# Hybrid decoder block on one core: softmax statistics merged on 16 partitions, and squares of q and k summed from two fp32r parts

## What is computed

```python
hmix = rmsnorm(x, norm_mix_g); proj = hmix @ w_in
q = rmsnorm(qkv[:, :, 0], q_norm_g) * scale      # per head, 64 channels: needs the sum of squares
k = rmsnorm(qkv[:, :, 1], k_norm_g)
for g, (window, dilation) in enumerate(((128, 1), (512, 4), (2048, 16))):
    o_g, lse_g = dilated_window_attention(q[g], k[g], v[g], slopes[g], window, dilation)
wgt = softmax(stack(lses), axis=0)                # over the three patterns, per token and head
o_attn = sum(wgt[..., None] * stack(outs), axis=0)
```

## Time and profile before

| what | us |
|---|---|
| median of 3 runs | 1832.22 (1832.21 to 1833.08) |
| time of the profiled execution | 1834.04 |
| its span, first to last instruction | 1832.2 |
| TensorE busy in the span | 1787.6 (98%) |
| mean granted TensorE clock | 0.994 |

### The profile page before, as it was taken

The page is one execution under the profiler, slowest core; times in us unless marked ns, Lnnn a source line. Parts: engine busy times, 40 slices in busy tenths (PEclk is TensorE's granted clock), DMA queues, the critical chain, the costliest instruction groups (busy, mean ns, idle before and its releaser), DMA issues.

```text
span 1832.2 us, 23655 instructions
## 1 busy us (share of the span) xinstructions
PE 1787.6 (98%) x8628; PEld 1420.1 (78%) x8628; DVE 1023.9 (56%) x1545; ACT 562.1 (31%) x1069; POOL 828.9 (45%) x597
## 2 busy tenths in 40 slices
PE   8999999999999987999999999999999999999997
PEld 6777777777777766788888888788888888888786
DVE  6336645564655489343313323787787887544644
ACT  6533444354245423111411222533333333000000
POOL 7536443644544274664225734265455454222221
PEclk9999999999999999999999999999999999999999
DMA  4111111211121023444411244322222232445211
GB/s 173 36 41 48 52 53 41 64 53 41 41 58 47 24 70 91 107 116 123 165 58 70 93 145 167 135 86 87 69 96 76 69 103 92 138 150 193 81 55 49
DMA packets 64194, 158.11 MB, mean 86 GB/s; under 512 B 10912, under 2 KB 27680, under 8 KB 64112
## 3 DMA queue, kind: packets, MB, share of 16 engines
q1 hardware_dynamic: 51856, 145.35, 24.4%
q10 hardware_dynamic: 11792, 10.04, 2.0%
q0 software_dynamic: 464, 1.62, 0.2%
HBM read 123.54 MB, written 32.26 MB: 85 GB/s over the span
## 4 chain that ended last, share of the span: by engine, by line
PE 88%; DVE 7%; POOL 1%; issue 1%; DMA 1%; ACT 1%; SPq 0%; DVEq 0%; POOLq 0%
PE bank L911 14%; PE bank L913 13%; PE bank L912 13%; PE bank L1274 7%; PE bank L1276 7%; PE bank L1275 7%; PE bank L1332 4%; PE bank L1334 4%; PE bank L1333 4%; PE bank L925 2%; PE bank L1059 2%; PE bank L1072 2%; PE bank L1045 2%; DVE run_z L1772 1%; PE bank L1238 1%
## 5 line engine op out<-in xcount | busy, mean ns | idle before, releaser
L911 PE MATMUL bank<-hhi,whi 128*128 128x512 f32 x1024 | 420.7, 411 | 5.8 <-DVE hlo L1709 4.0
L912 PE MATMUL bank<-hlo,whi 128*128 128x512 f32 x1024 | 404.9, 395 | 0.0
L913 PE MATMUL bank<-hhi,wlo 128*128 128x512 f32 x1024 | 404.8, 395 | 0.0
L626 POOL TENSOR_TENSOR wlo<-raw,whi 128x1024 fp32r<-128x1024 f32 (+1 forms) x84 | 197.5, 2351 | 293.1 <-DVE whi L1665 291.1
L911 PEld LDWEIGHTS bank<-hhi,whi 128*128 128x128 f32 x1024 | 193.7, 189 | 52.9 <-issue 8.7
L913 PEld LDWEIGHTS bank<-hhi,wlo 128*128 128x128 f32 x1024 | 193.5, 189 | 45.5
L912 PEld LDWEIGHTS bank<-hlo,whi 128*128 128x128 f32 x1024 | 194.2, 190 | 39.7 <-issue 1.2
L1822 DVE CUSTOM_DVE_ANT_0 sp<-bank,mask 128x128 f32<-128x128 f32 (+1 forms) x192 | 56.3, 349 | 113.7 <-PE bank L1045 111.8
L1447 ACT ACTIVATE sp<-sp,negm 128x128 f32<-128x128 f32 (+1 forms) x192 | 83.9, 440 | 107.5 <-DVE negm L1826 107.4
L884 POOL TENSOR_TENSOR plo<-st,phi 128x512 fp32r<-128x512 f32 x60 | 79.6, 1328 | 58.6 <-ACT phi L1577 57.4
L2113 DVE CAST fhi<-ff 128x1024 fp32r (+1 forms) x44 | 31.4, 715 | 125.5 <-PE bank L1334 125.5
(11 more groups left out here) (304 smaller groups left out, 3924.5 us busy)
## 6 DMA issues: line engine op xcount, KB each, us to landing
raw<-in_wblocks SPq DMA_DIRECT2D x98, 512.0 KB, 3.7
pair<-in_wblocks SPq DMA_DIRECT2D x40, 512.0 KB, 4.8
ff_scr<-ffo SPq DMA_DIRECT2D x22, 512.0 KB, 5.8
ff<-ff_scr SPq DMA_DIRECT2D x22, 512.0 KB, 4.0
rt<-rt_scr SPq DMA_DIRECT2D x8, 516.0 KB, 6.8
x<-in_xT SPq DMA_DIRECT2D x8, 512.0 KB, 8.8
zb_scr<-zb SPq DMA_DIRECT2D x8, 512.0 KB, 3.5
zb<-zb_scr SPq DMA_DIRECT2D x8, 512.0 KB, 3.4
```

The costliest lines, as they stand in the source:

```text
L626: pool.tensor_tensor(wlo[par][:, 0:cols], raw[par][:, 0:cols], whi[par][:, 0:cols].bitcast(F32), ALU.subtract).then_inc(lo_done, 1)
L911: nc.tensor.matmul(ps, a, x, start=start and k == k_list[0], stop=False)
L912: nc.tensor.matmul(ps, a, y, start=False, stop=False)
L913: last = nc.tensor.matmul(ps, b, x, start=False, stop=stop and k == k_list[-1])
```

## The change

It has two parts.

**Statistics.** Negated maxima and sums are kept in one tile `sd`, [128, 32], and PE transposes it in one transpose at j = 8, into [32, 128]. ACT copies that to `st_t`, and SP writes it to DRAM and reads it back (`spread`) as 16 rows (two heads by 8 pieces of 128 tokens): one store and four loads per attention, with the gather of the dilated order in the addresses. The merge of maxima and sums, the Exp of the two weights and the division by z are done on [16, 128] and [16, 256] tiles (`merge_max`, `merge_sum`, `weights_exp`). SP writes the weights to DRAM and loads them broadcast, in two DMAs of 64 partitions by 2 x 1024, into `ab` (`weights`); that is once for ag = 1 and once for ag = 2. `merge_psum` (DVE, one product, j 3 and 5) and `rescale`, `weigh` (POOL, j 4 and 6) now take place in the next slot; `normalise`, `merge_z`, `reciprocal_z` and the statistics' copies and 16 transposes are gone. The spreads stand in SP's list between the weight loads. After the last slot `taps(0)` is behind the second gate product, and `rotate(0)` is split in two around `gated(0, 0)`.

**Squares.** ACT computes each square twice, once rounded to fp32r (`sqh`) and once in float32 (`sq`); DVE subtracts (`square_lo`, j 2, 4, 6, 8) into `sql`, and PE sums both with two fp32r matmuls at j 3, 5, 7, 9 in place of one float32 matmul at j 2, 4, 6, 8. `rnorm` and `qk_scale` move one sub-step on with it.

```diff
+    ab = sb("ab", [P, 2, T])
     num = sb("num", [P, T])
-    ab_h0 = sb("ab_h0", [P, 2, HT])
+    sqh = sb("sqh", [P, 2, HT], F32R)
     t_num = sb("t_num", [P, 2, HT])
-    t_z = sb("t_z", [P, HT])
+    sql = sb("sql", [P, HT], F32R)
...
+    sd = sb("sd", [P, 2, 2, 8])
     utmp = sb("utmp", [P, CH, NCH])
-    rtmp = sb("rtmp", [P, 2, GB, NCH // 2])
-    hx = sb("hx", [P, T])
+    seed_t = sb("seed_t", [P, T])
+    st_t = sb("st_t", [P, P])
+    run, new, wgt = (sb(x, [P, 2, P]) for x in ("run", "new", "wgt"))
+    ones_r = sb("ones_r", [P, P], F32R)
...
@@ -444,16 +456,63 @@
             sp_.dma_start(rt[NST * u:NST * (u + 1)],
                           rt_scr.rearrange("(b g) s a k -> b s g a k", g=GB)[it]).then_inc(rt_in, 16)
+    def spread(a, hp, ag):
+        sp_.wait_ge(st_copied, a + 1)
+        if a:
+            sp_.wait_ge(new_in, 64 * a)
+        sp_.dma_start(stat_scr.rearrange("i x (s q) -> (i x s) q", q=P), st_t[0:32, :]).then_inc(st_out, 16)
+        sp_.wait_ge(st_out, 16 * (a + 1))
+        if merge_no(hp, ag) > 0:
+            sp_.wait_ge(wgt_done, 2 * hp if ag == 0 else merge_no(hp, ag))
+        for i in range(2):
+            for x in range(2):
+                to = (run if ag == 0 else new)[KC * x:KC * (x + 1), i, :]
+                sp_.dma_start(to.rearrange("c (r k) -> c r k", r=DIL[ag]),
+                              stat_scr[i, x].rearrange("(r c k) -> c r k", r=DIL[ag], c=KC)).then_inc(new_in, 16)
+        if ag:
+            weights(merge_no(hp, ag))
+    def weights(m):
+        sp_.wait_ge(wgt_done, m + 1)
+        if m:
+            sp_.wait_ge(ab_in, 32 * m)
+        sp_.dma_start(wgt_scr.rearrange("i x (c q) -> (x c) i q", q=P), wgt[0:2 * KC]).then_inc(wgt_out, 16)
+        sp_.wait_ge(wgt_out, 16 * (m + 1))
+        sp_.wait_ge(merged, 2 * m + 2)
+        for x in range(2):
+            sp_.dma_start(ab[DH * x:DH * (x + 1)], wgt_scr[:, x].unsqueeze(0).broadcast_to([DH, 2, T])).then_inc(ab_in, 16)
+    def loop_load(hp, b):
+        load(B_ALOOP + 10 * hp + b, wblocks[B_ALOOP + 10 * hp + b], (b + 1) % 2)
     for hp in range(HP - 1):
-        for b in range(10):
-            load(B_ALOOP + 10 * hp + b, wblocks[B_ALOOP + 10 * hp + b], (b + 1) % 2)
...
         save_u(hp)
         sp_.wait_ge(rot_done, hp + 1)
         for u in range(2):
...
+    spread(LAST - 3, HP - 2, 2)
+    for n in range(B_AEND + 3, B_AEND + 6):
+        load(n, wblocks[n], n % 2)
+    spread(LAST - 2, HP - 1, 0)
+    for n in range(B_AEND + 6, B_E1 + 1):
...
     sp_.wait_ge(pool_dma, 16 * HP)
     for q in range(HP - 1):
         if q == 2:
+            spread(LAST, HP - 1, 2)
...
         qk_scale(0, 0, 0, 3)
         ssm_signs()
-    def rescale(ag, hp, h):
+    def rescale(a, ag, hp, h):
         nm = natural(num[:, :], ag, h)
-        pool.wait_ge(ab_exp, hpc(hp, ag) + h + 1)
-        chain.link(pool.tensor_tensor(nm, nm, split2(ab[h][:, 0, :], ag), ALU.mult))
+        if ag == 1:
+            pool.wait_ge(d_read, 2 * a + 1)
+        else:
+            pool.wait_ge(merged, 2 * merge_no(hp, ag) + 2)
+        pool.wait_ge(ab_in, 32 * (merge_no(hp, ag) + 1))
+        chain.link(pool.tensor_tensor(nm, nm, natural(ab[:, 0, :], ag, h), ALU.mult))
     def weigh(a, ag, hp, h):
         nm = natural(num[:, :], ag, h)
...
-                pool.wait_ge(o_ready, 2 * hp)
+            if n is not None and j in (4, 6, 8, 10):
+                qk_scale(n, g, b, (j - 4) // 2)
+            if a and ag != 1 and j in (4, 6):
+                pg, ph, h = (ag + 2) % 3, hp - (ag == 0), j // 2 - 2
+                rescale(a - 1, pg, ph, h)
+                weigh(a - 1, pg, ph, h)
+            if a and ag == 0 and j == 7:
...
+        if n is None:
+            for h in range(2):
+                rescale(a, ag, hp, h)
+                weigh(a, ag, hp, h)
...
     def sum_squares(n, gi):
-        pe.wait_ge(sq_done, 4 * n + gi + 1)
-        nc.tensor.matmul(b_nb[:], blk_ones, sq[:, gi % 2, :], start=True, stop=True).then_inc(ss_done, 1)
+        pe.wait_ge(sql_done, 4 * n + gi + 1)
+        nc.tensor.matmul(b_nb[:], ones_r[:], sqh[:, gi % 2, :], start=True, stop=False)
+        nc.tensor.matmul(b_nb[:], ones_r[:], sql[:], start=False, stop=True).then_inc(ss_done, 1)
...
-            if n is not None and j in (2, 4, 6, 8):
-                gi = (j - 2) // 2
+            if n is not None and j in (3, 5, 7, 9):
+                gi = (j - 3) // 2
                 if gi == 0:
                     pe.wait_ge(vev_done, 2 * a + 2)
+                elif gi == 3:
+                    pe.wait_ge(st_copied, a + 1)
...
-                pe.wait_ge(stat_done, 2 * a + h + 1)
-                if h:
-                    pe.wait_ge(m_read, 2 * a + 2)
-                elif n is not None:
...
+                pe.wait_ge(exp_done, 8 * a + 8)
+                pe.wait_ge(ln_done, 4 * n + 3 if n is not None else 48)
+                nc.tensor.transpose(b_nb[0:32, 0:P], sd[:].rearrange("p i x s -> p (i x s)"), ident).then_inc(mt_done, 1)
             if a is not None:
...
-    pe.wait_ge(d_read, 2 * 12 + 1)
+    pe.wait_ge(tev, 8 * 12)
     tables(0, first=True)
-    taps(0)
     gate(1, 1, 1, 0)
     gate(1, 1, 1, 1)
+    pe.wait_ge(d_read, 2 * 12 + 1)
+    taps(0)
     chunk_inputs(0)
...
-        act.activation(sq[:, gi % 2, :].rearrange("p (i r) -> p i r", r=DIL[g]),
-                       by_residue((qn if gi < 2 else kn)[g][:, :], g, gi % 2), ACT.Square).then_inc(sq_done, 1)
+        x = by_residue((qn if gi < 2 else kn)[g][:, :], g, gi % 2)
+        act.activation(sqh[:, gi % 2, :].rearrange("p (i r) -> p i r", r=DIL[g]), x, ACT.Square)
+        act.activation(sq[:, gi % 2, :].rearrange("p (i r) -> p i r", r=DIL[g]), x, ACT.Square).then_inc(sq_done, 1)
...
+    def weights_exp(hp, ag):
+        act.wait_ge(wgt_in, merge_no(hp, ag) + 1)
+        act.activation(wgt[0:2 * KC], wgt[0:2 * KC], ACT.Exp).then_inc(wgt_exp, 1)
...
+            if a and ag != 1 and j == 0:
+                weights_exp(hp - (ag == 0), (ag + 2) % 3)
...
+            if a is not None and j == 8:
+                act.wait_ge(mt_done, a + 1)
+                if a:
+                    act.wait_ge(st_out, 16 * a)
+                act.activation(st_t[0:32, :], b_nb[0:32, 0:P], ACT.Copy).then_inc(st_copied, 1)
+            if n is not None and j in (3, 5, 7, 9):
+                rnorm(n, (j - 3) // 2, True)
...
+    def merge_max(a, ag, hp):
+        m = merge_no(hp, ag)
+        dve.wait_ge(new_in, 64 * (a + 1))
+        if m:
+            dve.wait_ge(wgt_out, 16 * m)
+        rn_, nn, up = by_token(run[:, 0], ag), in_chunk(new[:, 0], ag), by_token(wgt[:, 1], ag)
+        link(TT(up, rn_, nn, ALU.subtract))
+        link(TT(rn_, rn_, nn, ALU.min))
+        down, up = wgt[0:2 * KC, 0], wgt[0:2 * KC, 1]
         link(V.tensor_scalar(down, up, -1.0, 0.0, ALU.mult, ALU.min))
-        V.tensor_scalar(up, up, 0.0, None, ALU.min).then_inc(ab_in, 1)
+        V.tensor_scalar(up, up, 0.0, None, ALU.min).then_inc(wgt_in, 1)
+    def merge_sum(a, ag, hp):
+        m = merge_no(hp, ag)
+        dve.wait_ge(wgt_exp, m + 1)
+        rz_, nz, up = by_token(run[:, 1], ag), in_chunk(new[:, 1], ag), by_token(wgt[:, 1], ag)
+        z, both = run[0:2 * KC, 1], wgt[0:2 * KC]
+        TT(nz, nz, up, ALU.mult)
+        link(TT(z, z, both[:, 0], ALU.mult))
+        last = TT(rz_, rz_, nz, ALU.add)
+        if ag == NPAT - 1:
+            link(last)
+            link(V.reciprocal(z, z))
+            last = TT(both, both, z.unsqueeze(1).broadcast_to([2 * KC, 2, P]), ALU.mult)
+        last.then_inc(wgt_done, 1)
...
-        dve.wait_ge(ab_exp, 4 * hp + 2 * (ag - 1) + h + 1)
-        TT(t_num[:, h, :], b_o[h][:], ab[h][:, 1, :], ALU.mult)
-        TT(t_z[:], b_t[:], ab[h][:, 1, :], ALU.mult).then_inc(d_read, 1)
-
...
+        m = merge_no(hp, ag)
+        dve.wait_ge(merged, 2 * m + h + 1)
+        dve.wait_ge(ab_in, 32 * (m + 1))
+        TT(split2(t_num[:, h, :], ag), split2(b_o[h][:], ag), natural(ab[:, 1, :], ag, h), ALU.mult).then_inc(d_read, 1)
...
+    def square_lo(n, gi):
+        dve.wait_ge(sq_done, 4 * n + gi + 1)
+        if n or gi:
+            dve.wait_ge(ss_done, 4 * n + gi)
+        TT(sql[:], sq[:, gi % 2, :], sqh[:, gi % 2, :].bitcast(F32), ALU.subtract).then_inc(sql_done, 1)
...
+        square_lo(0, 0)
         evict(0, 0, 4, b_o[0])
+        square_lo(0, 1)
+        square_lo(0, 2)
         evict(0, 0, 5, b_o[1])
+        square_lo(0, 3)
...
+            if n is not None and j in (2, 4, 6, 8):
+                square_lo(n, j // 2 - 1)
...
+            if a and ag != 1 and j == 0:
+                merge_max(a - 1, (ag + 2) % 3, hp - (ag == 0))
...
+            if a and j in (3, 5):
+                merge_psum(a - 1, (ag + 2) % 3, hp - (ag == 0), j // 5)
...
-                h = j - 8
-                dve.wait_ge(exp_done, 8 * a + 4 * h + 4)
-                for i, x in enumerate((negm, den)):
```

(34 more changed lines are left out.)

158 lines of the change are left out of this document (45 added, 113 removed).

## The result

| | before | after |
|---|---|---|
| median of the runs, us | 1832.65 (1832.21 to 1835.24) | 1819.29 (1815.55 to 1820.91) |
| profiled execution, span, us | 1832.2 | 1817.5 (time 1819.81) |

The ratio is 0.9922, with a 95% interval of 0.991 to 0.9934: 13.4 us gained, where 36 were forecast, outside the range of 1781 to 1815.

A forecast was written before the change was run, and what follows sets the result against it. PE, busy for 98% of the span, was taken as the bound; -20.7 - 17.3 - 5.3 + 7.2 + 1.5 + 0.7 - 2.5 = -36.4 us from 1832.22 gave 1796 us, with an 8-in-10 range of 1781 to 1815.

The forecast's parts named there:

- The fp32r sum: PE, slots 1 to 11: two fp32r matmuls replace one float32 sum, saving 0.47 us each, 44 sums: -20.7 us.
- the transposes: PE, slots 1 to 11: one statistics transpose replaces four groups of four, 1.57 us a slot: -17.3 us.
- the gate at j = 8: PE waits 0.9 us at j = 8 for ACT's Ln, behind two squares, in eight slots: +7.2 us.
- the sums' new place: Slots with ag = 0: run_z work gone and sums a sub-step later, so PE's waits for squares go: -5.3 us.
- The cover is 7 us at least. Four of five loads aren't touched, so 0: SP's queue: weight loads held behind the waits in spread and weights still arrive before they are needed: 0 us.
- Seven such merges: 0 to 1 us each: PE's wait at j = 4 probabilities-times-v for merge weights coming through DRAM, mostly 0.2 us each: +1.5 us.
- my own trip of 16 to 19 us: Merge weights through DRAM to DVE's product end 16 to 19 us into the slot; PE needs the bank after 18 to 19.
- Rival 3: Weights late at j = 4: PE waits 6.5 us in each of 7 merges and 8 at the end, 1850 us; chance 0.07.
- I take -2.5: End of stage, last slot's start to PE resuming after rt: -2.5 us, with ends of -6 to +10.
- rival 2: DVE and POOL block each other at square_lo: 1 us reaches PE in each of 11 slots and the last, 1808; chance 0.17.
- ACT ... costs nothing but the wait above.: ACT's 44 second squares, 1.05 us or less, stay below half its time and add only the j = 8 wait.
- four signs of being wrong: Profile after: PE idle before probabilities-times-v; DVE subtractions over 2 us with PE waiting; PE waiting for wlo; end over 76 us.

The follow-up runs named there:

- three: mt_late, gp_late and merge_early together, on the changed kernel: 1794.79 us, 0.9796 of the kernel before.
- hold: Changed kernel with SP waiting for ab's landing ahead of save_u and the rt0 stores: 1813.32 us, 0.9896 of the kernel before.
- merge_early: Changed kernel with merge_max, merge_sum and weights_exp for ag = 1 moved from j == 0 of the next slot to j == 11 of their own: 1807.21 us, 0.9858.
- gp_late: Changed kernel with POOL's gp_table(0) moved behind the last slot and a wait for the last merge's weights: 1813.05 us, 0.9882 of the kernel before.
- copy_first: On three, ACT's copy of the transposed probabilities put ahead of its two squares at j = 3, 5, 7: 1795.41 us, 0.9789 of the kernel before.
- dve_cast: On three with the last num *= ab on DVE (1791.23 us): first Square dropped, DVE rounds sq to sqh; 1796.63 us, 0.9798.
- mt_late: Changed kernel with PE's statistics transpose at j == 8 moved behind that sub-step's probabilities-times-v and probabilities' transposes: 1806.21 us, 0.9858 of the kernel before.
- one_square: Changed kernel with one Square, one float32 matmul at sub-steps 3, 5, 7, 9 and no square_lo: 1820.88 us, 0.9926 of the kernel before.
- sp_order: Changed kernel with SP's stores of utmp and rt0 issued ahead of the wait for the merge's weights: 1823.2 us, 0.9949 of the kernel before.

## Why the prediction was wrong

**Right.** The fp32r sum, 0.46 to 0.47 us against 0.95; the transposes; the gate at j = 8, 8 x 1.0 us (7.0 of idle time in its row) for a forecast of 7.2; that the sums' new place takes away the waits for squares. The first, the last and the ag = 1 slots come out within 0.5 us of their forecast each, and with gate and late weights gone (three) the slots with ag = 1 and 2 fall by 3.1 and 3.2 us, for 3.45 that PE's terms give.

**"The cover is 7 us at least. Four of five loads aren't touched, so 0", and "Seven such merges: 0 to 1 us each".** This is the first step that failed. I followed the weight load behind SP's new wait, but not `save_u` and the two stores of `rt0` behind that load. Once SP is released they go out in one burst behind `ab`, which DVE then gets 9.0 us (issue at 174.29), 10.7 us (331.58) and 7.6 us (492.23) later, where I had 4.4 to 7.5 with the issue. In hold, without the burst, it is 7.4 to 7.8. And there was no spare time: my own trip of 16 to 19 us met a need at 18 to 19, and in the third of these slots, where the burst cost next to nothing, DVE's product ended at 500.89, only 0.1 us before PE used the bank. Slots with ag = 2 lost 8 us to it. The last slot stalls too, 3.17 us from start to start, but not by the burst: no stores stand behind its `ab`, which takes 7.5 us, and hold leaves 3.04. PE comes for it 14.7 us after that slot's start (639.98), where it is 18.0 in a full slot (339.17), since part of its sub-steps have no projection; my need at 18 to 19 was a full slot's. hold (-6.0) prices the burst, merge_early (-12.1) the whole lateness. Rival 3 had the right place and mechanism, but was priced for a doubled trip in each of seven merges. It came to some 10 us instead of 54, and turned no sign.

**"I take -2.5" for the end.** It was +4.1. The DVE merge was put at 3 us and took 10.8, because POOL makes a table beside it; I had the row for that the earlier trace rows and used it only for square_lo, in rival 2. The last slot's stall for `ab` brought DVE to the merge at 39.5 us, where I had 35 (34.2 in three, which has no such stall). So the weights left at 50.3 us, behind the free `ab` that I had rightly put at 48, and the loads took 7.6 us in place of 5. PE resumes 80.3 us after the slot's start for a forecast of 72.3. Each cause alone is worth most of the miss: gp_late takes 5.0 us off this stretch, merge_early 4.2, and three, with both, 8.8.

**"ACT ... costs nothing but the wait above."** In slots with ag = 0 both squares of a strided q or k take 1.1 us and stand ahead of a copy that PE waits for. ACT, then DVE, then POOL of the kernel after:
```profile
228.20 1.11 ACT L1432 ACTIVATE sqh<-qn 128x512 fp32r<-128x512 f32 x1
229.21 1.11 ACT L1433 ACTIVATE sq<-qn 128x512 f32<-128x512 f32 x1
230.22 0.58 ACT L1481 ACTIVATE ptr<-bank 128x512 f32<-128x512 f32 x1
...
230.35 2.77 DVE L1830 TENSOR_TENSOR sql<-sq,sqh 128x512 fp32r<-128x512 f32 x1 [0.22 <-ACT sq L1433]
...
234.53 2.18 DVE L1880 TENSOR_SCALAR sd<-mx 128x4 f32<-128x4 f32 x1
...
230.21 2.37 POOL L686 TENSOR_TENSOR wlo<-raw,whi 128x1024 fp32r<-128x1024 f32 x1 [6.15 <-DVE whi L1704]
...
234.53 2.15 POOL L831 TENSOR_TENSOR num<-num,ab 128x512 f32<-128x512 f32 x1
```
PE wanted that copy 0.7 us sooner; 10 us later the same happens with k, 1.1 us. On DVE a negation of four numbers per partition takes 2.18 us beside `rescale`, and the Exp that follows is as much later. This is rival 2, in the slots with ag = 0 alone, and mostly in two of the three (52.0 us each; the third, 50.6, waits 0.2 us for such a copy). No run takes POOL's work out of these slots, so how their 4 us divide between ACT and POOL isn't shown. ACT's second square and POOL's hold on DVE both stand in that chain: copy_first and dve_cast each took one link away, and neither made these slots shorter. A mean busy share of 32% for ACT said nothing about an order with no slack in one sub-step.

**The chances.** "Faster" was right. The range ended at 1815 because the unknown end (up to +10), rival 2 (+12) and rival 3 were priced one at a time. They came together, each at part of its price. Three of the four signs of being wrong that the prediction named are in the profile: idle time before probabilities-times-v, subtractions over 2 us, and an end longer than 76 us. PE never waited for `wlo` in the slots.

The Trainium skill (SBUF — State Buffer, Who interferes with whom) lets a VectorE instruction block behind GpSimd when it has two SBUF inputs or is a copy, cast or tensor_scalar in a two-port mode. The rows agree, down to operations on 16 partitions: 2.33 against 0.22 us; whether that tensor_scalar ran in such a mode no run here shows. By the Trainium skill (DMA: Bandwidth & Descriptors, on where the 2 us go) a small transfer costs some 2 us; the rows have 1.4 for 16 KB of `wgt_scr` and 2.7 for 16 KB of `stat_scr`, and 4.0 behind a burst.

What stays open: how the stall for `ab` comes to differ by a factor of three between slots whose queues look alike (45.5, 50.6, 44.1), and so how much of mt_late's 13 us is its own. With one square the late transpose has no gate to take away, and yet its profile has 0.6 us of stalls for `ab` in slots 1 to 11 where one_square's has 5.6.

## What to carry to other kernels

When a wait is put into a queue, list everything issued behind it up to the next wait: it leaves as one burst, just as the transfer that you wait for is under way. Starting the chain sooner (merge_early, 12 us) beats reordering the queue (hold, 6 us; sp_order, a loss). Work taken off the busiest engine is worth its time only once the gates that it brings are gone: here 1.6 us as it was made and 11.8 with the transpose late. A short chain of small DVE operations has to be priced with what POOL does in the same microseconds.
